# Head outputs evicted from PSUM by ScalarE instead of VectorE in a 56-unit attention stage

## The chip, the cores and the metric

The kernel runs on one core of one Trainium2 chip. The metric is device time in microseconds. Engines are named as in the profile: PE is TensorE (PEld its weight loads), DVE is VectorE, ACT is ScalarE, POOL is GpSimd, SP issues most DMAs.

## The reference

Two layers over 256 tokens of width 2048, all in fp32. Each layer is a projection, an attention stage with four kinds of heads, an output projection, a layer norm, a product-key expert layer over 16384 experts, and a second layer norm. Cut to what matters:

```python
def hybrid_mixer(x, w_in, sinks, lam_p, sub_g, w_out, layer_idx, cos, sin):
    proj = jnp.einsum('bld,dk->blk', x, w_in)
    ...
    oa = (acc * (corr / den)[..., None])      # A: 8 heads, window of 128, with sinks
    ob = diff_attention(...)                  # B: 4 heads of 128 columns, two softmaxes each
    ob = ob * lax.rsqrt(jnp.mean(jnp.square(ob), -1, keepdims=True) + RMS_EPS) * ...
    oc = num / den[..., None]                 # C: 8 heads, mixture of dilations
    od = dsa_attention(...)                   # D: 8 heads over the 64 keys an indexer picks
    mixed = jnp.concatenate([merge(oa), merge(ob), merge(oc), merge(od)], -1)
    return jnp.einsum('blk,kd->bld', mixed, w_out)
```

## The kernel before

Every weight matrix is streamed from HBM in tiles of 1 MB. ACT rounds each half tile to a high part (`split_hi`, L636), DVE forms the low part (`split_lo`, L919), and PE multiplies by both. These streams take nearly all of the time; the change touches only the attention stage between the input projection and the output projection, which runs once in each of the two layers.

The attention stage works through 56 units, one per head and block of 128 queries: 0 to 15 are the A heads, 16 to 23 the B heads, 24 to 39 the C heads, 40 to 55 the D heads. Even units have 128 keys, odd units 256. Each engine has its own list of instructions in program order, written out by hand, and semaphores tie them together. In step `u` of the loop the engines do this, in this order:

- PE: `scores(u+2)` (L442); `turn_probs(u)`: three transposes of the identity whose result nobody reads (L450), then the transposes of the probabilities (L456), which wait for the exponentials of unit u; `values(u-1)` (L469) into bank 6 or 7 by turns; and in units 0 to 15 `indexer_scores(u)` (L430) into the same two banks by turns.
- ACT: the exponentials of unit u+1 (L692, with a read of the accumulator, and in A units a sink term, L695); the copy of the transposed probabilities of unit u out of PSUM (L709); in units 0 to 15 the `relu` of the indexer's scores (L683), which waits for `indexer_scores(u)`; after unit 38 a square root; after units 40, 43, 46 and 49 one `split_hi` of the coming stream.
- DVE: mask and row maximum of unit u+1 (L1045), row sums of unit u (L1065, L1067 or L1071), the bias of the exponentials (L1053), the finishing of the probabilities with the reciprocal of the row sum (L1089), **the eviction of the output of unit u-2** (`take_out`, L1104 with 64 columns, L1100 with 128 for B heads), `indexer_add(u-1)` (L1005), a step of the indexer's top-k (L1028, L1030) at 17, 19, 21 and at every unit from 23 to 37, and a sum of squares (L1113) in units 28 to 35.

Two lines of PE say what waits for an eviction. In `indexer_scores(k)`, since it overwrites the bank in which the output of unit k-2 lies:

```python
if k >= 2:
    pe.wait_ge(irelu, k - 1)
    pe.wait_ge(head_out, k - 1)
```

and in `values(u)`, for the same reason, `pe.wait_ge(head_out, u - 1)`. `head_out` counts evicted outputs; with `k - 1` of them, unit k-2 has been evicted.

Of the kernel before, what the change touches and what calls it, by code (L numbers as in the profile page):

```python
# [20 lines left out]
HD = 64  # L21
# [67 lines left out]
def build(nc, x_in, w_in, w_out, wq, keys, u_t, v_t, ln, sinks, lamp, subg, layer_consts,  # L89
# [6 lines left out]
    with ExitStack() as ctx:  # L96
# [102 lines left out]
        def sem(name):  # L199
            s = ctx.enter_context(nc.semaphore(name))  # L200
            sems.append(s)
            return s
# [8 lines left out]
        scored, masked_done, nbias_done = sem("scored"), sem("masked_done"), sem("nbias_done")  # L211
        exp_done, sink_exp = sem("exp_done"), sem("sink_exp")
        mixed_probs, p_turned, p_stored = sem("mixed_probs"), sem("p_turned"), sem("p_stored")
        pv_done, head_out = sem("pv_done"), sem("head_out")
        rms_sum, rms_root, rms_scaled, mixed_done = sem("rms_sum"), sem("rms_root"), sem("rms_scaled"), sem("mixed_done")
        lam_sum, lam_exp = sem("lam_sum"), sem("lam_exp")
        out_evac = sem("out_evac")
# [32 lines left out]
        with nc.Fori(0, DEPTH) as layer:  # L250
# [7 lines left out]
            with nc.Block() as block:  # L258
# [367 lines left out]
                def _(act):  # L626
                    def split_hi(at, i, j, first=False):

                        if at == AT_IN and isinstance(i, int) and i == 0:
                            act.wait_ge(first_in[j // 2], layer * 16 + 16)  # L630
                        else:
                            act.wait_ge(raw_in[j // 2], i * 16 + at // BODY * 16)
                        if not first:
                            act.wait_ge(half_used, i * BODY + (at + j + 1 - NSPLIT))
                        half = raw[j // 2][:, (j % 2) * HT:(j % 2 + 1) * HT]
                        act.activation(hi[j % NSPLIT][:], half, ACT.Copy).then_inc(hi_done, 1)  # L636
# [48 lines left out]
                    def exps(u):  # L685
                        kind, h, b, items = UNITS[u]
                        K = (b + 1) * P
                        for n in items:
# [5 lines left out]
                            if kind == "A":  # L694
                                act.activation(small[:, 16 + n:17 + n], sinks_b[:, h:h + 1], ACT.Exp,  # L695
                                               bias=st[:, 1, n:n + 1]).then_inc(sink_exp, 1)

                    def unit_of(n):
                        return next(i for i, w in enumerate(UNITS) if n in w[3])

                    exps(0)
                    for u in range(n_units):
                        if u + 1 < n_units:
                            exps(u + 1)
                        K = (UNITS[u][2] + 1) * P
                        act.wait_ge(p_turned, u + 1)
                        if u >= 2:
                            act.wait_ge(pv_done, u - 1)
                        act.activation(probs_t[u % 2][:, 0:K], bank[4 + u % 2][:, 0:K], ACT.Copy).then_inc(p_stored, 1)  # L709
                        if u < N_IHEADS:  # L710
                            indexer_relu(u)
                        if u == AT_ROOT:

                            act.wait_ge(rms_sum, 8)
                            act.activation(small[:, 48:56], small[:, 40:48], ACT.Sqrt, bias=lay_b[:, 2:3],
                                           scale=1.0 / (2 * HD)).then_inc(rms_root, 1)
                        if u in SPLIT_UNITS:
                            split_hi(AT_OUT, 0, SPLIT_UNITS.index(u))
                    turn_high(1)
                    for m in range(NSPLIT, N_OUT):  # L720
                        split_hi(AT_OUT, m // BODY, m % BODY)
# [181 lines left out]
                def _(dve):  # L903
# [8 lines left out]
                    def own(n):  # L912
                        dve.wait_ge(dve_step, n)
# [138 lines left out]
                            dve.wait_ge(masked_done, i + 1)  # L1052
                            dve.tensor_scalar(st[:, 1, i:i + 1], st[:, 0, i:i + 1], -SCALE, None, ALU.mult).then_inc(nbias_done, 1)  # L1053

                    inverse = {}

                    def sums(u):

                        kind, h, b, items = UNITS[u]
# [13 lines left out]
                    def finish_probs(u, n):  # L1073

                        kind, h, b, items = UNITS[u]
                        K = (b + 1) * P
                        i = items[0]
                        if kind in "AB":
                            own(n)
                        if kind == "B":  # L1080
                            j = items[1]
                            own(mark(dve.tensor_scalar(probs[j % 4][:, 0:K], probs[j % 4][:, 0:K], st[:, 3, j:j + 1], neg_lam,
                                                       ALU.mult, ALU.mult)))
                            dve.scalar_tensor_tensor(out=probs[i % 4][:, 0:K], in0=probs[i % 4][:, 0:K], scalar=st[:, 3, i:i + 1],
                                                     in1=probs[j % 4][:, 0:K], op0=ALU.mult, op1=ALU.add).then_inc(mixed_probs, 1)
                            return
                        if kind == "C":
                            dve.wait_ge(mixed_probs, n_mixed(u))
                        inverse[u] = mark(dve.reciprocal(st[:, 3, i:i + 1], st[:, 2, i:i + 1]))  # L1089

                    def n_mixed(u):
                        return sum(UNITS[i][0] in "BC" for i in range(u + 1))

                    def take_out(u):
                        kind, h, b, items = UNITS[u]
                        dve.wait_ge(pv_done, u + 1)
                        src = bank[6 + u % 2]
                        if kind == "B":
                            at = MIX_B + 2 * HD * h
                            dve.tensor_copy(mixed[:, b, at:at + 2 * HD], src[:, 0:2 * HD]).then_inc(head_out, 1)  # L1100
                        else:
                            at = {"A": MIX_A, "C": MIX_C, "D": MIX_D}[kind] + HD * h
                            own(inverse[u])
                            dve.tensor_scalar(mixed[:, b, at:at + HD], src[:, 0:HD], st[:, 3, items[0]:items[0] + 1], None,  # L1104
                                              ALU.mult).then_inc(head_out, 1)


                    def square_sum(j):
                        h, b = j // 2, j % 2
# [14 lines left out]

                    row_max(0)
                    exp_bias(0)
                    for u in range(n_units + 2):
                        if u + 1 < n_units:
                            row_max(u + 1)
                        if u < n_units:  # L1130
                            n = sums(u)
                        if u + 1 < n_units:
                            exp_bias(u + 1)
                        if u < n_units:
                            finish_probs(u, n)
                        if u >= 2:
                            take_out(u - 2)
                        if 0 <= u - 1 < N_IHEADS:
                            indexer_add(u - 1)
                        if u in TOP_UNITS:  # L1140
                            top_round(TOP_UNITS.index(u))
                        if 0 <= u - AT_SQUARES < 8:
                            square_sum(u - AT_SQUARES)
                        if u == AT_ROOT + 3:
                            dve.wait_ge(rms_root, 1)
                            own(mark(dve.reciprocal(small[:, 40:48], small[:, 48:56])))
                        if 0 <= u - (AT_ROOT + 4) < 8:
                            rms_scale(u - (AT_ROOT + 4))
                        if u - 2 in SPLIT_UNITS:
                            split_lo(AT_OUT, 0, SPLIT_UNITS.index(u - 2))  # L1150
# [336 lines left out]
```

## Time and profile before

| | before |
|---|---|
| three timed runs | 4147.15, 4147.17, 4158.34 us; median 4147.17 |
| profiled execution | 4133.71 us, span 4131.7 us |
| PE busy | 3997.2 us (97%) |
| DVE busy | 2685.6 us (65%) |
| ACT busy | 1975.3 us (48%) |
| POOL busy | 516.8 us (13%) |

Busy time counts arithmetic, not semaphores or the issue of DMAs. The attention stage of the first layer lies between 246 and 343 us of the span, that of the second between 2326 and 2403 for its later units and a little before for the first ones. An engine's busy share over the whole span says little about that stage, in which the three engines hand small tiles to each other.

### The profile page before, as it was taken

The numbers are of one execution on the slowest core, as the hardware profiler recorded it, in microseconds if no ns is written. First come the engines' busy times: TensorE is split into PE (matmuls) and PEld (weight loads), VectorE is DVE, ScalarE is ACT, GpSimd is POOL, SyncE is SP. The second block draws the span as 40 slices with busy tenths as digits, with TensorE's granted clock in tenths as the row PEclk, the third lists the DMA queues.
The fourth block names the chain that finished last, engine by engine and source line by source line (L and its number), as shares of the span: only waits on it lengthen the run. The fifth ranks groups of instructions, "written<-read, shape, count | busy, mean of one in ns | idle before, by whom it ended". The sixth has DMA issues, their size and how long they took to land.

```text
span 4131.7 us, 65461 instructions
## 1 busy us (share of the span) xinstructions
PE 3997.2 (97%) x20692; PEld 3384.3 (82%) x20692; DVE 2685.6 (65%) x5308; ACT 1975.3 (48%) x2824; POOL 516.8 (13%) x728
## 2 busy tenths in 40 slices
PE   8999899999999999999899998999999999999997
PEld 7877788888888888888678777888888888888886
DVE  5665568667866555555656755686688665555556
ACT  4454344555455444444344543445554554444443
POOL 0100000451055000000001000004500540000000
PEclk9999999999999999999999998999999999999998
DMA  6523455558655666666445144555586456666664
GB/s 220 189 71 128 169 183 206 183 183 264 219 182 190 222 229 249 229 229 229 171 172 192 53 166 150 178 206 182 183 272 215 176 180 235 229 249 229 229 229 178
DMA packets 243055, 810.78 MB, mean 196 GB/s; under 512 B 24320, under 2 KB 157440, under 8 KB 157440
## 3 DMA queue, kind: packets, MB, share of 16 engines
q1 hardware_dynamic: 206080, 775.78, 53.6%
q10 hardware_dynamic: 36864, 33.57, 2.3%
q8 instruction: 64, 1.05, 0.1%
q14 instruction: 47, 0.39, 0.0%
HBM read 756.82 MB, written 52.43 MB: 196 GB/s over the span
## 4 chain that ended last, share of the span: by engine, by line
PE 43%; DVE 5%; issue 1%; ACT 1%; DVEq 0%; ACTq 0%
PE bank L371 10%; PE bank L592 6%; PE bank L594 6%; PE bank L593 6%; PE bank L372 5%; PE bank L383 2%; PE bank L385 2%; PE bank L384 2%; DVE lo L919 2%; PE bank L553 1%; DVE top_i L1248 0%; PE bank L450 0%; DVE top_v L1247 0%; DVE x L1182 0%; ACT hi L636 0%
## 5 line engine op out<-in xcount | busy, mean ns | idle before, releaser
L919 DVE TENSOR_TENSOR lo<-raw,hi 128x1024 fp32r<-128x1024 f32 x1312 | 1640.5, 1252 | 1197.5 <-ACT hi L636 1168.8
L636 ACT ACTIVATE hi<-raw 128x1024 fp32r<-128x1024 f32 x1312 | 1388.4, 1059 | 1369.7 <-PE bank L594 759.1
L371 PE MATMUL bank<-xhl,hi 128*128 128x512 f32 x4608 | 1642.7, 400 | 5.2 <-DVE xhl L925 2.8
L372 PE MATMUL bank<-xhl,lo 128*128 128x256 f32 x4608 | 1293.9, 281 | 0.0
L371 PEld LDWEIGHTS bank<-xhl,hi 128*128 128x128 f32 x4608 | 869.5, 189 | 211.0 <-DVE gelu_out L1225 3.9
L372 PEld LDWEIGHTS bank<-xhl,lo 128*128 128x128 f32 x4608 | 874.6, 190 | 0.0
L592 PE MATMUL bank<-hi,xhl 128*128 128x512 f32 x2048 | 797.1, 389 | 2.2 <-DVE gelu_out L1225 1.9
L593 PE MATMUL bank<-lo,xhl 128*128 128x512 f32 x2048 | 796.7, 389 | 0.0
L594 PE MATMUL bank<-hi,xhl 128*128 128x512 f32 x2048 | 796.7, 389 | 0.0
L592 PEld LDWEIGHTS bank<-hi,xhl 128*128 128x128 f32 x2048 | 384.4, 188 | 83.3 <-DVE gelu_out L1225 2.5
L594 PEld LDWEIGHTS bank<-hi,xhl 128*128 128x128 f32 x2048 | 384.4, 188 | 79.8
L593 PEld LDWEIGHTS bank<-lo,xhl 128*128 128x128 f32 x2048 | 384.4, 188 | 79.7
L866 POOL TENSOR_SCALAR scr<-iota_k,small 128x128 f32<-128x128 f32 x512 | 406.4, 810 | 12.3
L383 PE MATMUL bank<-hi,xhl 128*128 128x512 f32 (+1 forms) x896 | 353.1, 394 | 9.5 <-DVE lo L919 6.1
L385 PE MATMUL bank<-hi,xhl 128*128 128x512 f32 (+1 forms) x896 | 350.1, 391 | 0.0
L384 PE MATMUL bank<-lo,xhl 128*128 128x512 f32 (+1 forms) x896 | 350.1, 391 | 0.0
L876 POOL TENSOR_TENSOR x<-x,arena 128x512 f32<-128x512 f32 x8 | 13.4, 1681 | 1889.5 <-ACT x L733 1889.5
L756 ACT ACTIVATE gelu_out<-bank 128x256 f32<-128x256 f32 x256 | 97.0, 379 | 262.2 <-PE bank L372 262.0
L761 ACT ACTIVATE gelu_out<-gelu_out 128x256 f32<-128x256 f32 x256 | 105.9, 414 | 238.3 <-DVE gelu_out L1225 238.2
L383 PEld LDWEIGHTS bank<-hi,xhl 128*128 128x128 f32 x896 | 169.6, 189 | 43.8 <-issue 6.5
L385 PEld LDWEIGHTS bank<-hi,xhl 128*128 128x128 f32 x896 | 169.6, 189 | 34.7
L384 PEld LDWEIGHTS bank<-lo,xhl 128*128 128x128 f32 x896 | 169.8, 189 | 33.4
(133 smaller groups left out, 2592.2 us busy)
## 6 DMA issues: line engine op xcount, KB each, us to landing
raw<-u_t SPq DMA_DIRECT2D x256, 1024.0 KB, 4.8
raw<-v_t SPq DMA_DIRECT2D x256, 1024.0 KB, 4.8
raw<-w_in SPq DMA_DIRECT2D x84, 1024.0 KB, 4.8
raw<-w_out SPq DMA_DIRECT2D x32, 1024.0 KB, 4.8
raw<-wq SPq DMA_DIRECT2D x32, 1024.0 KB, 4.8
gelu_scratch<-gelu_out ACTq DMA_DIRECT2D x256, 128.0 KB, 1.7
scr<-gelu_scratch SPq DMA_DIRECT2D x256, 128.0 KB, 4.6
gates_scratch<-arena SPq DMA_DIRECT2D x32, 512.0 KB, 9.9
```

The lines of the kernel that those rows point to most:

```text
L371: pe.matmul(acc[:], wh, xhl[:, c, :, :].rearrange("p a t -> p (a t)"), start=(c == 0), stop=False)
L372: return pe.matmul(acc[:, L:2 * L], wl, xh[:, c, :], start=False, stop=(c == DC - 1))
L383: pe.matmul(banks[b][:, 0:width], st_h, mh, start=(c == first_c), stop=False)
L384: pe.matmul(banks[b][:, 0:width], st_h, ml, start=False, stop=False)
L385: last = pe.matmul(banks[b][:, 0:width], st_l, mh, start=False, stop=(c == last_c))
L592: pe.matmul(y, a_h, vh, start=start, stop=False)
L593: pe.matmul(y, a_h, vl, start=False, stop=False)
L594: last = pe.matmul(y, a_l, vh, start=False, stop=stop)
L636: act.activation(hi[j % NSPLIT][:], half, ACT.Copy).then_inc(hi_done, 1)
L761: act.activation(gelu_out[m % 2][:], gelu_out[m % 2][:], ACT.Gelu).then_inc(gelu_done, 1)
L866: last = pool.tensor_scalar(oh1[p][:, t, :], iota_k[:], key_cols[p][:, t:t + 1], None, ALU.is_equal)
L919: dve.tensor_tensor(lo[j % NSPLIT][:], half, hi[j % NSPLIT][:].bitcast(F32), ALU.subtract).then_inc(lo_done, 1)
```

## The change

`take_out` leaves DVE's list and enters ACT's. On ACT it stands in step u behind the copy of the transposed probabilities and ahead of the indexer's `relu`, and evicts unit u-2; the last two evictions follow the loop. For B heads it is a plain copy of 128 columns, for the others a copy of 64 columns whose scale is the column of reciprocals. The reciprocals stay on DVE and now count a semaphore, `inverted`, for which ACT waits. PE's list is the same.

```diff
+                    def take_out(u):
+                        kind, h, b, items = UNITS[u]
+                        act.wait_ge(pv_done, u + 1)
+                        src = bank[6 + u % 2]
+                        if kind == "B":
+                            at = MIX_B + 2 * HD * h
+                            act.activation(mixed[:, b, at:at + 2 * HD], src[:, 0:2 * HD], ACT.Copy).then_inc(head_out, 1)
+                        else:
+                            at = {"A": MIX_A, "C": MIX_C, "D": MIX_D}[kind] + HD * h
+                            act.wait_ge(inverted, n_inverted(u))
+                            act.activation(mixed[:, b, at:at + HD], src[:, 0:HD], ACT.Copy,
+                                           scale=st[:, 3, items[0]:items[0] + 1]).then_inc(head_out, 1)
...
                         act.activation(probs_t[u % 2][:, 0:K], bank[4 + u % 2][:, 0:K], ACT.Copy).then_inc(p_stored, 1)
+                        if u >= 2:
+                            take_out(u - 2)
                         if u < N_IHEADS:
                             indexer_relu(u)
...
+                    take_out(n_units - 2)
+                    take_out(n_units - 1)
                     turn_high(1)
...
-                        inverse[u] = mark(dve.reciprocal(st[:, 3, i:i + 1], st[:, 2, i:i + 1]))
+                        dve.reciprocal(st[:, 3, i:i + 1], st[:, 2, i:i + 1]).then_inc(inverted, 1)
...
-                        dve.wait_ge(pv_done, u + 1)
-                        src = bank[6 + u % 2]
...
-                            dve.tensor_copy(mixed[:, b, at:at + 2 * HD], src[:, 0:2 * HD]).then_inc(head_out, 1)
...
-                            own(inverse[u])
-                            dve.tensor_scalar(mixed[:, b, at:at + HD], src[:, 0:HD], st[:, 3, items[0]:items[0] + 1], None,
-                                              ALU.mult).then_inc(head_out, 1)
...
-                    for u in range(n_units + 2):
+                    for u in range(n_units):
...
-                        if u >= 2:
-                            take_out(u - 2)
```

ACT's list around units 8 and 9, as a difference from before (L709 of before is L725 now; L683 is the indexer's relu):

```order
 L695 ACTIVATE small<-par,st 128x1
-L709 ACTIVATE scr<-bank4 128x128
+L725 ACTIVATE scr<-bank4 128x128
+L711 ACTIVATE arena<-bank6,st 128x64
 L683 ACTIVATE scr<-bank6 128x256
 L692 ACTIVATE scr,st<-scr,st 128x128
 L695 ACTIVATE small<-par,st 128x1
-L709 ACTIVATE scr<-bank5 128x256
+L725 ACTIVATE scr<-bank5 128x256
+L711 ACTIVATE arena<-bank7,st 128x64
 L683 ACTIVATE scr<-bank7 128x256
```

The eviction has come in between the copy and the relu of each step. It reads the bank that the relu's own input is then written to.

PE's list at the same place, unchanged, with the semaphores that each instruction waits for:

```order
L456 MATMUL bank5<-ident,scr 128x128 [waits exp_done]
L456 MATMUL bank5<-ident,scr 128x128
L469 MATMUL bank6<-arena,scr 128x64 [waits irelu,head_out,p_stored]
L430 MATMUL bank7<-arena 128x256 [waits head_out,irelu]
L442 MATMUL bank0<-arena 128x128 [waits masked_done]
```

L430 waits for `head_out` as before, but what counts `head_out` now stands behind ACT's copy of the step; L442 and everything after it stand behind L430.

DVE's list in a C unit that also carries a top-k step and a sum of squares, before:

```order
L1067 SCALAR_TENSOR_TENSOR scr,st<-scr,arena 128x128
L1053 TENSOR_SCALAR st<-st 128x1
L1089 RECIPROCAL st<-st 128x1
L1104 TENSOR_SCALAR arena<-bank6,st 128x64
L1028 MAX small<-scr 128x8 x2
L1113 ISA scr,small<-arena 128x128
```

and now, where 20 lines have been added ahead of it (L1067 reads L1085, and so on):

```order
L1085 SCALAR_TENSOR_TENSOR scr,st<-scr,arena 128x128
L1073 TENSOR_SCALAR st<-st 128x1
L1107 RECIPROCAL st<-st 128x1
L1048 MAX small<-scr 128x8 x2
L1117 ISA scr,small<-arena 128x128
```

One instruction is gone, and nothing else has moved.

## Rows read from the trace of the kernel before

**Rows 1.** Windows, first layer's attention; engines' busy us (x instructions), then PEclk.

```profile
246.00:275.00 29.00, 28.51 (x194) 21.71 (x192) 21.26 (x123) 20.93 (x86) 0.00 (x0) 1.00 0.00 1
275.00:290.00 15.00, 12.39 (x80) 8.16 (x79) 14.34 (x79) 9.90 (x38) 0.00 (x0) 1.00 0.01 2
290.00:318.00 28.00, 26.24 (x161) 19.25 (x161) 26.97 (x176) 13.98 (x49) 0.00 (x0) 1.00 0.00 1
```

**Rows 2.** Timeline, units 9 to 11: start us, duration us, engine, line.

```profile
263.31 0.37 ACT L709 ACTIVATE scr<-bank 128x256 f32<-128x256 f32 x1
...
263.33 0.48 PE L430 MATMUL bank<-arena 64*128 64x256 f32 x1
...
264.06 0.38 ACT L683 ACTIVATE scr<-bank 128x256 f32<-128x256 f32 x1 [0.38 <-PE bank L430]
...
264.34 0.50 ACT L692 ACTIVATE scr<-scr,st 128x256 f32<-128x256 f32 x1
...
265.02 0.26 ACT L709 ACTIVATE scr<-bank 128x128 f32<-128x128 f32 x1
...
265.15 0.70 PE L430 MATMUL bank<-arena 64*128 64x256 f32 x2
...
266.59 0.38 PE L456 MATMUL bank<-ident,scr 128*128 128x128 f32 x2
...
267.01 0.39 ACT L709 ACTIVATE scr<-bank 128x256 f32<-128x256 f32 x1 [0.18 <-PE bank L456]
```

**Rows 3.** Timeline, unit 2's indexer and what follows; last row: unit 15's indexer.

```profile
252.06 0.49 PE L430 MATMUL bank<-arena 64*128 64x128 f32 x2
...
252.58 0.28 ACT L683 ACTIVATE scr<-bank 128x128 f32<-128x128 f32 x1 [0.39 <-PE bank L430]
252.75 0.39 ACT L692 ACTIVATE scr<-scr,st 128x128 f32<-128x128 f32 x1
...
253.71 0.39 ACT L709 ACTIVATE scr<-bank 128x256 f32<-128x256 f32 x1 [0.29 <-PE bank L456]
...
274.25 0.48 PE L430 MATMUL bank<-arena 64*128 64x256 f32 x1
```

**Rows 4.** Groups by form, ACT, attention of the first layer: busy us, mean ns.

```profile
L692 ACT ACTIVATE scr<-scr,st 128x256 f32<-128x256 f32 x32 | 16.1, 503 | 11.6 <-DVE st L1053 11.6
L692 ACT ACTIVATE scr<-scr,st 128x128 f32<-128x128 f32 x32 | 12.7, 397 | 9.7 <-DVE st L1053 9.4
...
L709 ACT ACTIVATE scr<-bank 128x128 f32<-128x128 f32 x28 | 7.3, 261 | 0.3 <-PE bank L456 0.3
```

**Rows 5.** Timeline, DVE in unit 30: eviction and the instruction after it.

```profile
301.47 0.28 DVE L1104 TENSOR_SCALAR arena<-bank,st 128x64 f32<-128x64 f32 x1
...
301.67 0.28 DVE L1028 MAX8 small<-scr 128x8 f32<-128x128 f32 x1
```

**Rows 6.** Timeline, ACT's copies of units 24, 28 and 36.

```profile
292.09 0.26 ACT L709 ACTIVATE scr<-bank 128x128 f32<-128x128 f32 x1
...
298.21 0.25 ACT L709 ACTIVATE scr<-bank 128x128 f32<-128x128 f32 x1
...
313.21 0.26 ACT L709 ACTIVATE scr<-bank 128x128 f32<-128x128 f32 x1
```

**Rows 7.** Timeline, PE, the identity transposes of units 41 and 43.

```profile
321.32 0.31 PEld L450 LDWEIGHTS bank<-ident 128*128 128x128 f32 x3 [0.33 <-issue]
...
324.20 0.31 PEld L450 LDWEIGHTS bank<-ident 128*128 128x128 f32 x3 [0.33 <-issue]
```

**Rows 8.** Timeline, the square root after unit 38 and PE's wait behind it.

```profile
316.38 1.28 ACT L715 ACT_TABLE_LOAD   x1
...
319.83 0.14 PEld L456 LDWEIGHTS bank<-ident,scr 128*128 128x128 f32 x1 [1.41 <-ACT scr L692]
```

**Rows 9.** Timeline, unit 47's copy, the next exponential, and `values(47)` on PE.

```profile
331.29 0.37 ACT L709 ACTIVATE scr<-bank 128x256 f32<-128x256 f32 x1
...
331.61 0.51 ACT L692 ACTIVATE scr<-scr,st 128x256 f32<-128x256 f32 x1
...
331.71 0.41 PEld L469 LDWEIGHTS bank<-arena,scr 128*128 128x128 f32 x3
```

**Rows 10.** Windows, around the first layer norm: columns as in Rows 1.

```profile
440.00:445.00 5.00, 0.00 (x0) 0.00 (x0) 4.47 (x10) 2.40 (x5) 2.27 (x2) 0.72 0.00 0
445.00:450.00 5.00, 2.48 (x11) 2.14 (x12) 5.00 (x4) 1.19 (x2) 4.24 (x3) 0.50 0.00 0
```

More of the change, by code:

```diff
@@ L213, in build @@
         mixed_probs, p_turned, p_stored = sem("mixed_probs"), sem("p_turned"), sem("p_stored")
-        pv_done, head_out = sem("pv_done"), sem("head_out")
+        pv_done, inverted, head_out = sem("pv_done"), sem("inverted"), sem("head_out")
         rms_sum, rms_root, rms_scaled, mixed_done = sem("rms_sum"), sem("rms_root"), sem("rms_scaled"), sem("mixed_done")
@@ L696, in exps, with n_inverted @@
                                                bias=st[:, 1, n:n + 1]).then_inc(sink_exp, 1)
+                    def n_inverted(u):
+                        return sum(UNITS[i][0] != "B" for i in range(u + 1))
+                    def take_out(u):
[10 more added lines that the diff above has]
+                                           scale=st[:, 3, items[0]:items[0] + 1]).then_inc(head_out, 1)
                     def unit_of(n):
@@ L1053, in exp_bias @@
                             dve.tensor_scalar(st[:, 1, i:i + 1], st[:, 0, i:i + 1], -SCALE, None, ALU.mult).then_inc(nbias_done, 1)
-                    inverse = {}
                     def sums(u):
@@ L1088, in finish_probs @@
                             dve.wait_ge(mixed_probs, n_mixed(u))
-                        inverse[u] = mark(dve.reciprocal(st[:, 3, i:i + 1], st[:, 2, i:i + 1]))
+                        dve.reciprocal(st[:, 3, i:i + 1], st[:, 2, i:i + 1]).then_inc(inverted, 1)
                     def n_mixed(u):
                         return sum(UNITS[i][0] in "BC" for i in range(u + 1))
-                    def take_out(u):
-                        kind, h, b, items = UNITS[u]
-                        dve.wait_ge(pv_done, u + 1)
-                        src = bank[6 + u % 2]
-                        if kind == "B":
-                            at = MIX_B + 2 * HD * h
-                            dve.tensor_copy(mixed[:, b, at:at + 2 * HD], src[:, 0:2 * HD]).then_inc(head_out, 1)
-                        else:
-                            at = {"A": MIX_A, "C": MIX_C, "D": MIX_D}[kind] + HD * h
-                            own(inverse[u])
-                            dve.tensor_scalar(mixed[:, b, at:at + HD], src[:, 0:HD], st[:, 3, items[0]:items[0] + 1], None,
-                                              ALU.mult).then_inc(head_out, 1)
                     def square_sum(j):
```

## The prediction

> **What bounds the kernel now.** I read the page first: PE is busy for 97% of the span, so time is won or lost only where PE waits or can be made to wait. The change touches the attention stage alone, so I cut that stage of the first layer into windows by kind of unit. In units 0 to 15 PE is busy for 28.51 of 29 us and is the bound. In the B units DVE is busy for 14.34 of 15 us and PE for 12.39; in units 23 to 38 DVE has 26.97 of 28 us, PE 26.24 and ACT only 13.98 [rows 1]. There DVE is the bound, or close to PE. So the work leaves an engine that matters from unit 16 on, and does not matter before.
>
> Then I read the timeline for what stands between the engines. In units 0 to 15 PE starts the indexer's scores of unit 9 at 263.33, almost together with ACT's copy at 263.31, and ACT's relu waits for them [rows 2]. Nothing that ACT does in that step holds PE back. That is what the change ends: `head_out` for unit u-2 was counted by DVE, long before PE came to `indexer_scores(u)`, and is now counted by ACT behind the copy of step u, which itself waits for PE's transposes of step u. PE must stand at L430 until ACT has copied and evicted, and everything behind L430 on PE (the scores, transposes and values of the next unit) stands with it.
>
> **The cost of one eviction on ACT.** No row shows a 64-column copy with a column as scale. An exponential, which also has a column as operand, takes 503 ns for 256 columns and 397 for 128 [rows 4]: 64 columns fewer are 53 ns less, so 0.34 us, which I take, since it has the same kind of operand. The lower bound is the plain copy from PSUM, 261 ns for 128 columns [rows 4], less the same 53: 0.21. The upper bound is the 128-column exponential itself, 0.40. For ACT's own list less counts, because an instruction starts about 0.10 us before the end of the one ahead (the relu of 0.28 at 252.58 is followed at 252.75 [rows 3]): 0.24.
>
> The Trainium skill, "ScalarE: Activation LUTs", section "What ACT_TABLE_LOAD costs", gives an ACTIVATE with immediate operands 186 ns plus 0.833 ns per column and each column operand 93 ns more. By that this one would take 0.33 us, an estimate from the page; at 128 columns with one such operand it gives 0.39, and the trace agrees with 397 ns. It would change the sum by 0.01 us in each of 14 units.
>
> **Units 2 to 15: a new loop.** The time from one `indexer_scores` to the next now runs: the scores, the relu, the next exponentials, the next copy, the eviction, and the signal to PE. The parts, for 256 indexer columns: scores to relu 0.73 (263.33 to 264.06), relu to exponential 0.28, exponential to copy 0.68 before an even unit's copy [rows 2], and 0.11 less before an odd one, by the difference of the two exponentials. For 128 columns: 0.52 and 0.17 [rows 3]. From the start of a copy to the next instruction on ACT I take 0.16 for 128 columns (0.26 less 0.10) and 0.32 for 256 (331.29 to 331.61 [rows 9]); then 0.34 for the eviction and 0.05 from ACT's end to PE's start (331.66 to 331.71 [rows 9]). So the tail from copy to `indexer_scores` is 0.55 into an even unit and 0.71 into an odd one.
>
> There is a second way round, through PE: from `indexer_scores(u)` over the next scores and transposes to the next copy. Where the scores use the same rows of the array as the indexer, the way into an odd unit is the longer: 265.15 to 267.01, 1.86 us [rows 2], or 252.06 to 253.71, 1.65 us, with 128 columns [rows 3]. Where they use different rows, ACT's way is longer. This makes, per unit:
>
> - 256 columns: three into even units, 0.73 + 0.28 + 0.68 + 0.55 = 2.24; two into odd ones by ACT's way, 0.73 + 0.28 + 0.57 + 0.71 = 2.29; two by PE's way, 1.86 + 0.71 = 2.57. Sum 16.4.
> - 128 columns: three even, 0.52 + 0.17 + 0.68 + 0.55 = 1.92; one odd by ACT's way, 1.97; two by PE's way, 1.65 + 0.71 = 2.36. Sum 12.4.
>
> Together 28.8 us for 13 steps, against 274.25 - 252.06 = 22.2 us now [rows 3]: 6.6 more. Unit 2 has a first stall of its own, about 0.4 by the same parts. So **+7.0 us per layer**, and ACT, PE and DVE are all late by it when the B units start, since the exponentials of unit 17 follow the relu of unit 15.
>
> **Units 16 to 38: DVE gives some back.** From the eviction's start to the next instruction DVE takes 0.20 us (301.47 to 301.67 [rows 5]); its own duration of 0.28 overlaps. In units 28 to 35, with top-k step and sum of squares, DVE has no gap: eight units take 15.00 us (298.21 to 313.21 [rows 6]), 3.75 a pair, while PE needs 2.88 a pair where nothing holds it (321.32 to 324.20 [rows 7]). All eight evictions count: 1.6. In units 24 to 27 a pair takes 3.06 (292.09 to 298.21 [rows 6]), so only 0.18 a pair can be had before PE's 2.88; with the pair before it 0.5. In the B units every second unit waits for the exponentials' end before its second row maximum, and DVE's list is the bound only in the other half: 4 x 0.20 = 0.8, with both ends 0 and 1.6. ACT's evictions fit in its idle time there: it is busy for 13.98 of 28 us [rows 1], and 16 x 0.24 is 3.8. So **-2.9 us per layer**. Without that idle time these evictions would cost up to 3.8.
>
> **Unit 38 to the end.** The square root's table load at 316.38 stands behind the eviction of unit 36, and PE waits for the exponential behind it at 319.83 [rows 8]: 0.24 later, less about 0.2 that a lighter DVE wins before it. `values(39)` and `values(47)` start right at the end of a copy (331.66 to 331.71 [rows 9]) and now also wait for the eviction behind it: 0.3 to 0.4 each. In the other D units PE is the bound and ACT is ahead. The last units, without scores on PE, run at the pace of copy and values: 0.4. Together **+1.1 us per layer**, with both ends 0 and 2.2.
>
> **Sum.** 7.0 - 2.9 + 1.1 = 5.2 us per layer, 10.4 us for both. The profiled execution would go from 4133.71 to 4144.1; the median of the timed runs stands 13.5 us above it, so the median becomes 4157.6 us, 0.25% more. A measurement of this kernel can tell about 0.3%, 12.4 us, from no change.
>
> **The rivals.**
>
> 1. The wait is hidden: the stall at L430 costs nothing because something else holds PE as long. It would need a second wait at the same place. The 0.18 and 0.29 us that ACT's copy waits for PE's transposes [rows 2, 3] show the opposite: PE is what ACT waits for, and it has 0.5 us idle in 29 [rows 1]. It would leave -2.9 + 1.1 per layer, so 4143.6.
> 2. Faster: the relief of DVE counts in every unit and ACT's new work lies in ACT's waits. For it: DVE's busy share from unit 16 on, and the 0.38 us that ACT waits for L430 [rows 2]. Then 112 x 0.20 = 22.4 us are won, 4124.8. It decides only if the eviction ends before PE reaches L430. ACT's copy of unit 9 starts when PE starts L430 [rows 2], so the eviction would have to come before the copy, which the order of ACT's list rules out.
> 3. Slower by clock: PE, now waiting in every unit, loses its full clock. At the first layer norm PE had nothing to do for 5 us, and the granted clock was 0.72 and then 0.50, the lower of its two levels of 1.2 and 2.4 GHz [rows 10]. Against it: in the B units PE was busy 12.39 of 15 us, in waits of under 1 us, at 1.00 [rows 1], and the new waits make it 28.5 of 36, much the same share. It decides once the rows show a clock under 0.9 in units 2 to 15. PE's 28.5 us of work there would double, some 20 us a layer beyond its waits: 4197. The Trainium skill, "TensorE: Matmul & The Clock Gate", Part 1, has the clock follow recent activity; [rows 1, 10] agree.
> 4. The same mechanism, but with no gift from DVE, because PE and ACT take over as bounds as soon as DVE is lighter: 7.0 + 1.1 per layer, 4163.4.
>
> **How the numbers follow.** My forecast, with cases of its size on both sides of it, 0.72; rival 1, 0.07; rival 2, 0.04; rival 3, 0.03; rival 4, 0.14. Bounds of the forecast: an eviction of 0.21 takes 13 x 2 x 0.13 + 0.3 = 3.7 us off, one of 0.40 adds 1.7; B units between 0 and 1.6 per layer move it by 1.6 either way; the last part between 0 and 2.2 by 2.2 either way. That makes 4150.1 to 4163.1. The range reaches on to rival 4 and a little beyond for the spread of the runs, 4148 to 4166. Over 0.3% slower is more than 4159.6: about 0.3 of the forecast's 0.72, all of rivals 3 and 4: 0.39. Faster by over 0.3% is rival 2 alone, 0.04. The rest, 0.57, is within 0.3%.
>
> **What would show it.** In the profile after, windows for units 0 to 15 would show some 36 us instead of 29 with PE busy about 28.5 and a clock of 1.00; the waits would have a row of L430, or its weight load, waiting for ACT's L711, some 0.5 us long, 14 times per layer; L711 would have a mean near 0.34 us. Units 28 to 36 would take about 13.4 us instead of 15.0. I am wrong if L430 waits for nothing, if its waits don't lengthen the units, or if the C units don't get shorter; and the size is off if L711's duration is nearer 0.21 or if unit 38's table load moves by more than 0.3.

## The result and the profile after

| | before | after |
|---|---|---|
| median of six timed runs | 4148.24 us (4147.15 to 4158.34) | 4185.31 us (4173.08 to 4192.14) |
| ratio, 95% interval | | 1.0083 (1.0061 to 1.0104) |
| profiled execution, mean granted clock | 4133.71 us, 0.985 | 4185.17 us, 0.973 |

The kernel became slower by 0.83%, 37 us where 10.4 were forecast, and the time lies outside the range. First the page of after: its span, its busy times and the row of PE's granted clock in 40 slices.

```profile
span 4183.2 us, 65461 instructions
...
PE 4041.1 (97%) x20692; PEld 3421.8 (82%) x20692; DVE 2666.6 (64%) x5196; ACT 2001.5 (48%) x2936; POOL 515.4 (12%) x728
...
PEclk9998899999999999999999989999999999999998
```

PE has the same 20692 instructions as before and is busy for 43.9 us more (4041.1 - 3997.2). No PE instruction was added, so PE ran more slowly somewhere. The clock row has an 8 in its fourth slice, 314 to 418 us, in which the first layer's attention stage ends; before's row has a 9 there.

I then cut the first layer's stage by units, from the start of ACT's copy of one unit to that of another: from the copy of unit 0 to that of unit 15, then to those of 23, 38, 40 and 55. Below I call these windows the A units, the B units, the C units, the wait at unit 40 (its copy comes right behind that wait) and the D units. These are the windows of before; the columns are the stretch, its length, busy time (instructions) of PE, PEld, DVE, ACT and POOL, PE's granted clock, DMA share and GB/s.

```profile
249.65:274.19 24.54, 24.38 (x170) 19.16 (x169) 18.86 (x106) 18.08 (x78) 0.00 (x0) 1.00 0.00 1
274.19:290.70 16.51, 13.90 (x92) 9.52 (x90) 15.85 (x90) 10.30 (x41) 0.00 (x0) 1.00 0.01 2
290.70:316.11 25.41, 23.65 (x145) 17.14 (x143) 25.09 (x164) 12.13 (x45) 0.00 (x0) 1.00 0.00 1
316.11:320.51 4.40, 3.23 (x21) 2.28 (x20) 1.78 (x12) 4.34 (x10) 0.00 (x0) 1.00 0.00 0
320.51:341.18 20.67, 20.67 (x141) 16.62 (x140) 16.79 (x83) 14.71 (x49) 0.00 (x0) 1.00 0.26 90
```

The same units in after:

```profile
249.86:284.66 34.80, 28.91 (x171) 22.30 (x169) 17.00 (x99) 20.97 (x90) 0.00 (x0) 0.86 0.00 1
284.66:302.64 17.98, 16.40 (x92) 12.02 (x91) 14.03 (x76) 11.64 (x48) 0.00 (x0) 0.79 0.00 1
302.64:325.14 22.50, 22.09 (x144) 17.06 (x142) 21.91 (x150) 15.38 (x61) 0.00 (x0) 1.00 0.01 2
325.14:329.90 4.76, 3.31 (x21) 2.32 (x19) 1.48 (x10) 4.70 (x12) 0.00 (x0) 0.98 0.00 0
329.90:367.50 37.60, 37.60 (x142) 30.16 (x141) 14.75 (x68) 17.82 (x65) 0.00 (x0) 0.50 0.15 56
```

The clock was 1.00 in all of before's stretches. Now it is 0.86, 0.79 and, in the D units, 0.50, half speed, which is 1.2 GHz in place of 2.4. The D units alone take 37.60 us instead of 20.67. The A units take 10.3 us more, of which a part is the stall that was forecast. Only the C units got shorter, as was thought, by 2.9 us. Lateness counts from the same copy in before. In the second layer the copy of unit 55 comes 53.7 us late and that of unit 0 27.6 us, so it lost 26.1 us too; the first lost 26.3.

The forecast stall stands in the timeline of after, units 10 and 11, and can be read against [rows 2].

```profile
269.43 0.26 ACT L725 ACTIVATE scr<-bank 128x128 f32<-128x128 f32 x1
...
269.59 0.31 ACT L711 ACTIVATE arena<-bank,st 128x64 f32<-128x64 f32 x1
...
270.04 0.67 PE L430 MATMUL bank<-arena 64*128 64x256 f32 x2 [0.41 <-ACT arena L711]
...
270.75 0.38 ACT L683 ACTIVATE scr<-bank 128x256 f32<-128x256 f32 x1 [0.85 <-PE bank L430]
```

Copy, eviction, PE's L430, and then ACT's own relu behind it: the loop of the prediction. By unit 12 ACT's copy is 5.5 us late, 5.3 of it since unit 0, all of it at full clock. Then the clock falls, in unit 13 (windows of after):

```profile
272.00:274.00 2.00, 1.40 (x11) 1.25 (x10) 0.59 (x6) 1.15 (x5) 0.00 (x0) 1.00 0.00 0
274.00:276.00 2.00, 1.59 (x10) 0.84 (x9) 0.83 (x6) 0.84 (x6) 0.00 (x0) 0.78 0.03 8
276.00:280.00 4.00, 3.55 (x16) 3.01 (x17) 1.56 (x7) 2.25 (x10) 0.00 (x0) 0.50 0.01 2
290.00:295.00 5.00, 5.00 (x32) 3.90 (x32) 3.89 (x24) 3.05 (x13) 0.00 (x0) 0.78 0.00 0
328.00:330.00 2.00, 0.67 (x3) 0.51 (x4) 0.42 (x4) 1.99 (x8) 0.00 (x0) 0.93 0.00 0
330.00:332.00 2.00, 2.00 (x7) 1.23 (x7) 0.35 (x4) 1.70 (x5) 0.00 (x0) 0.50 0.00 0
340.00:350.00 10.00, 10.00 (x38) 7.78 (x37) 5.43 (x21) 5.22 (x19) 0.00 (x0) 0.50 0.29 107
```

It comes back near 292, in the B units, and falls again just before 330. What PE did there is in the timeline around unit 40:

```profile
325.64 1.28 ACT L733 ACT_TABLE_LOAD   x1
...
328.55 0.40 ACT L692 ACTIVATE scr<-scr,st 128x128 f32<-128x128 f32 x1
...
329.09 0.33 PE L456 MATMUL bank<-ident,scr 128*128 128x128 f32 x1 [1.21 <-ACT scr L692]
...
329.66 1.04 PE L469 MATMUL bank<-arena,scr 128*128 128x64 f32 x4 [0.24 <-ACT arena L711]
...
331.77 0.90 PE L450 MATMUL bank<-ident 128*128 128x128 f32 x3
```

PE waits 1.21 us for the exponential behind the table loads, then 0.24 more for an eviction. The 1.41 us of [rows 8] are those of a weight load; the row of before that can be set beside these is that of PE:

```profile
319.84 0.33 PE L456 MATMUL bank<-ident,scr 128*128 128x128 f32 x1 [1.17 <-ACT scr L692]
```

In before no wait for an eviction follows. So from the copy of unit 38 to that of unit 40 PE is without work for 1.17 us in before and for 1.45 us in after. The three transposes of the identity took 0.55 us with the clock at 1.00 and take 0.90 here: the half clock. PE is busy for 10.00 of 10 us from 340 to 350, and the clock stays at 0.50.

What each eviction cost is close to what was foreseen. By its source line, in after:

```profile
L711 ACT ACTIVATE arena<-bank,st x96: 302/308/318, 252.3 to 2454.4; 128x64 f32<-128x64 f32 x96
...
  PE bank L430: 12.4, 26
  PE bank L469: 1.7, 4
```

The median is 308 ns. PE's L430 waited for it 26 times in two layers, 0.48 us each.

### The profile page after: what moved, and what is told of

Its sections match the earlier page's. It is cut to its first block and busy times, and to the rows that moved or that the text cites. A ratio compares the mean times of both kernels' runs of the same rounds, so it can differ in the third digit from the quotient of the medians.

```text
span 4183.2 us, 65461 instructions
## 1 busy us (share of the span) xinstructions
PE 4041.1 (97%) x20692; PEld 3421.8 (82%) x20692; DVE 2666.6 (64%) x5196; ACT 2001.5 (48%) x2936; POOL 515.4 (12%) x728
## 5 line engine op out<-in xcount | busy, mean ns | idle before, releaser
L383 PEld LDWEIGHTS bank<-hi,xhl 128*128 128x128 f32 x896 | 169.6, 189 | 43.9 <-issue 6.6
```

The lines of the kernel that those rows point to most:

```text
L383: pe.matmul(banks[b][:, 0:width], st_h, mh, start=(c == first_c), stop=False)
```

## The experiments

The theory that I took to the chip: the prediction's three terms hold, and the rest is PE's clock, lost in two places for two reasons. The idle times of units 2 to 15 do the one, the wait at unit 40 the other. The rivals were: the units grew for another reason and the clock only went with it; the clock falls because ACT evicts in the D units; and the D fall is a consequence of the one in the A units.

Times are medians; "before" stands for the kernel before, timed beside them 26, 26 and 17 times: 4147.98 for the first four kernels, 4147.99 for the next four, 4147.67 for the last three.

| run | median, us (lowest to highest, runs) | ratio to before, 95% | clock, profiled |
|---|---|---|---|
| e1_fill_A | 4171.00 (4169.27 to 4172.85, 5) | 1.0052 (1.0029 to 1.0076) | 0.978 |
| e2_fill_A_40 | 4138.94 (4135.37 to 4142.63, 10) | 0.9974 (0.9963 to 0.9985) | 0.987 |
| e3_early | 4151.27 (4132.27 to 4161.34, 10) | 1.0004 (0.9988 to 1.0021) | 0.985 |
| e4_A_on_dve | 4155.96 (4153.73 to 4159.27, 10) | 1.0018 (1.0002 to 1.0033) | 0.977 |
| e5_A_on_act | 4191.16 (4173.37 to 4193.94, 4) | 1.0096 (1.0066 to 1.0127) | 0.971 |
| e6_before_fill_40 | 4133.39 (4131.29 to 4138.00, 12) | 0.9969 (0.9954 to 0.9984) | 0.986 |
| e7_early_fill_40 | 4131.07 (4127.54 to 4134.53, 12) | 0.9967 (0.9955 to 0.9979) | 0.987 |
| e8_A_on_dve_fill_40 | 4126.67 (4124.99 to 4130.96, 9) | 0.9955 (0.9939 to 0.9971) | 0.988 |
| e9_more_in_D | 4175.89 (one execution) | | 0.979 |
| e10_after_fill_40 | 4157.26 (4151.77 to 4167.24, 10) | 1.0027 (1.0007 to 1.0046) | 0.980 |
| e11_only_16_37 | 4122.23 (4119.92 to 4127.49, 6) | 0.9934 (0.9913 to 0.9954) | 0.988 |

**Filling PE's waits: e1_fill_A, e2_fill_A_40, e10_after_fill_40.** e1 adds four transposes of the identity, which nobody reads, ahead of the wait at L430 in units 2 to 15. e10 leaves that out and puts 14 such transposes instead of 3 ahead of the wait at unit 40 (`AT_ROOT` is 38). e2 has both.

```diff
 # e1, e2: indexer_scores
+for _ in range(4 if k >= 2 else 0):
+    pe.transpose(bank[4 + (k + 1) % 2][:, W - P:W], ident[:], ident[:])
 # e2, e10: turn_probs
-for _ in range(3):
+for _ in range(14 if u == AT_ROOT + 2 else 3):
```

> The changed kernel with four more identity transposes on PE ahead of each indexer score of units 2 to 15, into a bank that nobody reads; they lie in the wait for ACT's eviction. Theory 'wait and clock': the units 2 to 15 keep a granted clock of 1.00 in both layers; the stalls themselves stay (about 7 us a layer more than before), but the 5 to 7 us a layer that PE loses there at half clock are gone; the D units, whose clock falls after unit 38, lose as much as in the changed kernel. Median about 4172 us. Rival 'waits alone': the clock is a side effect, the fillers only lengthen PE's list: 4185 us or more, with half clock still in units 13 to 17. A third outcome, if the fall in the D units is an aftermath of the one in the A units: both go, 4158 us.

> As the run before, and fourteen instead of three identity transposes on PE ahead of unit 40, where PE waits about 1.2 us for the exponential behind the table load. Theory 'wait and clock': the D units keep a clock of 1.00 too, and 26 to 28 us for both layers come back: about 4158 us, what the stalls alone were forecast to give. Rival, if the wait at unit 40 is not what lets the clock fall: D units at half clock as before, time equal to the run before.

> The changed kernel with fourteen transposes ahead of unit 40 and nothing in units 2 to 15. Theory 'wait and clock': the falls of the D units and of the A units are two separate ones. The D units keep 1.00 and give back some 15 us a layer; the A units still fall, 5 to 6 us a layer. Median about 4139 + 11 = 4150 us, granted clock 0.86 in units 0 to 15. Rival 'one chain': the D units still fall, since the A units did; 4180.

e1 took 14.3 us off after's time, and e10 28.1. The windows of e2, first layer, by the same units as above:

```profile
249.71:281.30 31.59, 30.42 (x224) 23.74 (x223) 15.99 (x92) 20.75 (x90) 0.00 (x0) 1.00 0.00 1
281.30:297.86 16.56, 14.16 (x96) 9.89 (x94) 14.91 (x83) 11.65 (x49) 0.00 (x0) 1.00 0.00 1
297.86:320.36 22.50, 22.09 (x144) 17.06 (x142) 21.91 (x150) 15.38 (x61) 0.00 (x0) 1.00 0.01 2
320.36:325.12 4.76, 4.51 (x32) 3.52 (x31) 1.47 (x10) 4.70 (x11) 0.00 (x0) 1.00 0.01 3
325.12:346.68 21.56, 21.16 (x142) 16.79 (x141) 13.96 (x68) 17.42 (x64) 0.00 (x0) 1.00 0.28 98
```

More work on PE, and the kernel is 46 us shorter than after: what the idle times did to the clock cost more than the idle times as such. Every eviction is where the change put it, and the clock is 1.00 throughout. So the second rival, ACT's evictions in the D units, falls. So does the first: with 56 transposes more, the A units take 31.59 us, not 34.80.

Of e1 the rows of the A units, of the wait at unit 40 and of the D units:

```profile
249.82:281.41 31.59, 30.41 (x224) 23.74 (x223) 15.99 (x92) 20.75 (x91) 0.00 (x0) 1.00 0.01 2
320.46:325.22 4.76, 3.31 (x21) 2.32 (x20) 1.47 (x10) 4.70 (x11) 0.00 (x0) 1.00 0.00 0
325.22:361.26 36.04, 36.04 (x142) 28.97 (x141) 14.65 (x68) 17.83 (x65) 0.00 (x0) 0.53 0.17 59
```

And of e10 those of the A and of the D units:

```profile
248.90:286.38 37.48, 32.14 (x171) 24.80 (x169) 17.02 (x99) 21.10 (x91) 0.00 (x0) 0.77 0.00 1
...
331.61:353.17 21.56, 21.16 (x142) 16.79 (x141) 13.97 (x68) 17.42 (x64) 0.00 (x0) 1.00 0.28 98
```

In e1 the A units kept the clock and the D units lost it; in e10 it was the other way round. So the D units fall without a fall in the A units, against the third rival.

**Who evicts where: e4_A_on_dve, e5_A_on_act.** Both give a set of units back to DVE, in DVE's old place, and leave the others on ACT; the second is the complement of the first.

```diff
+ON_DVE = range(0, 16)      # e5: range(16, 56)
...
-                        if u >= 2:
+                        if u >= 2 and u - 2 not in ON_DVE:
                             take_out(u - 2)
...
+                        if u >= 2 and u - 2 in ON_DVE:
+                            take_out_dve(u - 2)
```

> Only the evictions of units 16 to 55 are moved to ACT; those of units 0 to 15 stay on DVE. Theory 'wait and clock': units 0 to 15 as before, clock 1.00, no stall; units 16 to 38 win 3 to 4 us a layer; so about 4141 us, or 4167 us if the clock falls at unit 40 by itself. Rival 'waits alone': the evictions on ACT in the later units cost what they cost in the changed kernel, 26 us or more for both layers, with no fall of the clock.

> The other half: the evictions of units 0 to 15 on ACT, those of units 16 to 55 on DVE as before. Theory 'wait and clock': units 2 to 15 and the B units cost what they cost in the changed kernel, 12 to 13 us a layer, 7 of them stalls and the rest half clock; the D units, whose list on ACT is that of before, lose nothing if their fall came from the later evictions, so about 4147 + 25 = 4172 us. If the D units' clock depends only on the wait at unit 40, which this kernel has as well, it can fall there too, by chance of where it stands: up to 4195.

With the A evictions on DVE the A units took 24.53 us at 1.00, as before, so the stall and its clock fall belong to those evictions. The D units lost the clock all the same. In the windows of e4 (unit 40 starts at 317.03):

```profile
316.00:318.00 2.00, 1.54 (x7) 1.16 (x7) 0.74 (x7) 2.00 (x9) 0.00 (x0) 0.81 0.00 0
318.00:320.00 2.00, 2.00 (x9) 1.45 (x7) 1.14 (x6) 0.92 (x4) 0.00 (x0) 0.50 0.00 0
320.00:330.00 10.00, 10.00 (x37) 7.78 (x38) 5.23 (x22) 4.74 (x17) 0.00 (x0) 0.50 0.00 0
```

In e5 the D evictions were on DVE, the wait at unit 40 was before's in the first layer (PE busy for 3.23 of 4.40 us), and yet:

```profile
247.25:287.08 39.83, 35.40 (x170) 27.47 (x169) 17.04 (x99) 21.38 (x90) 0.00 (x0) 0.68 0.00 1
...
335.47:371.37 35.90, 35.90 (x141) 28.84 (x140) 18.78 (x83) 14.96 (x49) 0.00 (x0) 0.52 0.17 59
```

So even before's arrangement can fall in the D units. That led to the next runs. In the second layer of e5 the clock fell sooner, in unit 37, ahead of the square root:

```profile
2412.00:2414.00 2.00, 1.55 (x11) 1.13 (x11) 1.97 (x15) 0.87 (x4) 0.00 (x0) 1.00 0.00 0
2414.00:2416.00 2.00, 2.00 (x11) 1.60 (x11) 1.98 (x12) 1.11 (x5) 0.00 (x0) 0.76 0.00 0
```

PE's waits there, of up to 0.45 us, are for DVE, as in before, whose C units kept the clock in both layers of its profiled execution. So the wait at unit 40 is not the only place at which this stage can fall.

The A units have the same lists in after, e10, e9 and e5, and lose the clock at different times: in the first layer near 275 us in after (unit 13), near 269 in e10 (unit 11) and near 261 in e5 (unit 8). The sooner it fell, the longer they took: 34.80, 37.48 and 39.83 us.

**Does before itself lose the clock there? e6_before_fill_40, e8_A_on_dve_fill_40.** The 14 transposes at unit 40 (the second diff above) go into before, and into e4.

> The kernel before with fourteen instead of three identity transposes on PE ahead of unit 40. Theory: the spread of the kernel before, 4132 to 4163 us, is the clock falling in some executions after the wait at unit 40, for which its profiled execution of 4133.7 us is one without a fall. Then this kernel stays near the lower end: median 4133 to 4138, spread under 10 us, 0.3% faster than before. Rival: its spread comes from elsewhere, and the fill changes nothing (4148).

> Evictions of units 0 to 15 on DVE, those of units 16 to 55 on ACT, and the fourteen transposes ahead of unit 40. Theory: no stall in units 0 to 15, 3.3 us a layer won in units 16 to 38, 1.2 given back after them, no fall of the clock: 4 to 5 us under the kernel before with the same fill, about 4129 us, the fastest of all. Rival: the D units fall to half clock from the new waits behind the copies and not from the wait at unit 40; then 4156 as without the fill.

The kernel before gained 0.31% from eleven idle transposes, and e4 29.3 us. In e6 PE has no gap left at the wait; its row for the stretch from the copy of unit 38 to that of unit 40 reads:

```profile
313.71:318.11 4.40, 4.40 (x32) 3.48 (x31) 1.78 (x12) 4.34 (x11) 0.00 (x0) 1.00 0.00 0
```

The 69 runs of before fall into three groups: 17 from 4131.0 to 4138.4 at a mean clock of 0.984 to 0.986, 40 from 4143.7 to 4151.5 at 0.980 to 0.983, 12 from 4157.4 to 4165.6 at 0.977 to 0.980. Their means are 12.9 and 12.6 us apart. All twelve of e6 lie from 4131.3 to 4138.0, in the first group. So before loses the clock at unit 40 in neither, one or both of its layers, and one loss costs about 13 us. This is inferred from e6 and from the clocks: no profiled execution of before shows a fall, and in the traces of other kernels a fall lengthened the D units by 14.5 to 16.0 us. The profiled execution of before, 4133.71 us, on which the whole prediction was built, was one without any.

**The order on ACT: e3_early, e7_early_fill_40.** The eviction of unit u-2 goes ahead of the copy of unit u in ACT's list; it brings the wait for `pv_done` with it. e7 has the 14 transposes too.

```diff
-                        act.wait_ge(p_turned, u + 1)
-                        if u >= 2:
-                            act.wait_ge(pv_done, u - 1)
-                        act.activation(probs_t[u % 2][:, 0:K], bank[4 + u % 2][:, 0:K], ACT.Copy).then_inc(p_stored, 1)
                         if u >= 2:
                             take_out(u - 2)
+                        act.wait_ge(p_turned, u + 1)
+                        act.activation(probs_t[u % 2][:, 0:K], bank[4 + u % 2][:, 0:K], ACT.Copy).then_inc(p_stored, 1)
```

> The changed kernel with one move on ACT: the eviction of unit u-2 stands ahead of the copy of unit u, not behind it. Theory 'wait and clock': the stall of PE at the indexer score is gone, since the eviction no longer stands behind PE's transposes of the same unit; units 0 to 15 take 29 us a layer as before with clock 1.00, units 16 to 38 are 3 to 4 us shorter. If the D units' fall has its own cause at unit 40, they still lose 13 us a layer: about 4166 us; if it follows from the A units, about 4141 us. Rival 'ACT is too full': units 0 to 15 stay 5 us or more longer than before, since ACT's list is the bound.

> The early eviction on ACT (ahead of the copy) with the fourteen transposes ahead of unit 40. Theory: the traces of the early kernel stand 1.4 us a layer below the kernel before where no clock fell, and its spread of 4132 to 4161 us came from falls; with the fill the median is 4131 to 4136 us. Rival: the falls of the early kernel come from its units 0 to 15, where PE is busy for 24.96 of 27.45 us and not 24.38 of 24.54; then the spread stays and the median is near 4150.

In the timeline of e3, unit 12:

```profile
269.21 0.30 ACT L711 ACTIVATE arena<-bank,st 128x64 f32<-128x64 f32 x1
...
269.40 0.27 ACT L725 ACTIVATE scr<-bank 128x128 f32<-128x128 f32 x1
...
269.65 0.45 PE L430 MATMUL bank<-arena 64*128 64x256 f32 x1 [0.24 <-ACT arena L711]
```

The wait is 0.24 us instead of the 0.41 of after's unit 12, the A units take 27.45 us instead of 34.80, and they keep the clock. The stall was expected to be gone; it is only smaller, since before's A units took 24.54. The runs of e3 still spread from 4132.3 to 4161.3, and its median equals that of before. With the wait at unit 40 filled, e7, the highest run is 4134.5, so the spread came from the fall there. The median of e7 is 2.3 us under that of e6, but not through this stage: from the copy of unit 0 to that of unit 55 it takes 91.62 us in e7 and 91.54 in e6.

**What keeps the clock down in the D units? e9_more_in_D.** Five more idle transposes in each unit from 41 on, and none more at unit 40, so that the clock may fall as in after.

```diff
-for _ in range(3):
+for _ in range(3 if u <= AT_ROOT + 2 else 8):
```

> The changed kernel with eight instead of three identity transposes in each unit from 41 on and no fill at unit 40: can more work of the full array bring the clock back where the D units have fallen to the lower level with PE busy all the time? If it is the kind of work that keeps the level low, the clock is back at 1.00 a few units after the fall and units 40 to 55 take about 28 us, not 37.6. If not, they stay at 0.50 and take 37.6 + 15 x 5 x 0.11 x 2 = 54 us.

Windows of e9 behind its unit 40:

```profile
330.00:335.00 5.00, 3.55 (x15) 2.39 (x14) 1.44 (x12) 4.08 (x12) 0.00 (x0) 0.73 0.00 0
335.00:340.00 5.00, 5.00 (x25) 4.59 (x24) 2.12 (x7) 1.62 (x7) 0.00 (x0) 0.59 0.00 0
340.00:345.00 5.00, 5.00 (x37) 4.08 (x37) 2.44 (x11) 3.08 (x11) 0.00 (x0) 1.00 0.01 5
```

The clock fell near 332 and was back near 339. From the copy of unit 40 to that of unit 55 it took 31.97 us, with 75 more transposes, against 37.60; in the second layer 31.69 against 37.59. PE was busy for nearly all of the time in both kernels; what differed was what it was busy with. It is one execution, though with the same course in both layers.

**The version that follows: e11_only_16_37.** ACT evicts only units 16 to 37, where DVE is the bound; DVE keeps the others, and unit 40 has its 14 transposes.

```diff
+ON_DVE = [*range(0, 16), *range(38, 56)]
```

> Evictions on ACT in units 16 to 37 alone, on DVE in the others, and the fourteen transposes ahead of unit 40. Theory: the gain of units 16 to 38 stays (3.3 us a layer), the 1.2 us a layer that ACT's evictions cost from unit 38 on are gone: about 2 us under the version with only units 0 to 15 on DVE, 4124 to 4126 us. Rival: DVE's evictions in the D units cost what ACT's do; 4127, no difference.

It is 0.66% faster than before. Its D units:

```profile
317.19:338.00 20.81, 20.81 (x142) 16.76 (x141) 17.09 (x85) 14.71 (x49) 0.00 (x0) 1.00 0.26 90
```

That is 0.75 us less a layer than in e2, where `values` waited for evictions on ACT. About 15 of its 25 us come from the filled wait (e6: 14.6 us), which has nothing to do with the change. The evictions that were moved where they help shorten the stage by 2.81 us a layer against before's profiled execution (88.72 us from the copy of unit 0 to that of unit 55, against 91.53), 5.6 for both. The other 5 us or so lie outside the stage and are not explained.

**What was expected and missed.** e1, e6 and e7 came where they were expected. e2 came 19 us under its 4158, e4 11 us under its 4167 and e3 between its two numbers. These had been reckoned from before's median of 4147, which has the clock falls in it; without them before takes 4133. e10 came 7 us over its 4150, since the fall in its A units cost more than was allowed for. e8 and e11 came 2.3 and 1.8 us under, e5 near its upper end of 4195, and the D units of e9 took 32 us, not 28.

## Why the prediction was wrong

**The three terms were right in kind, and their sum was.** e2 is the change without a clock fall, with four idle transposes a unit added, which had lengthened it by 0.2 us at unit 12 (5.48 us late, 5.29 in after). Its copies against before's in the first layer, counted from unit 0: 7.7 us late at unit 16, where the B units start (forecast 7.0), 4.2 at unit 38 (so -3.5; forecast -2.9), 5.4 at unit 55 (so +1.25; forecast +1.1), together 5.4 a layer against 5.2. Both layers make 11.0 at the last unit. By medians against e6 it is only 5.6, and the profiled span is 9.1 longer than before's (4140.8 against 4131.7). The streams outside the stage differ by several us from kernel to kernel: from the end of the first layer's stage to the start of the second's (copy of unit 55 to copy of unit 0) it is 1962.5 us in e11 and 1970.7 in e6. I did not follow that up.

**So two terms were off and made up for each other:** the loop by 0.7 us a layer, what DVE gives back by 0.6. In e4, where no stall comes before them, units 16 to 38 won 3.3, and two sizes within that were off: the B units won 0.4 a layer, not 0.8, and units 28 to 35 won 2.3, not 1.6. Units 24 to 27 with the pair before them won 0.5, as forecast.

**The eviction** took 308 ns, not 0.34 us, well inside its bounds. The estimate of 0.33 from the Trainium skill, "ScalarE: Activation LUTs", section "What ACT_TABLE_LOAD costs", was nearer by 0.01 us and still 0.02 above the measurement.

**Two steps failed. The one in the A units was the dismissal of rival 3**, at a chance of 0.03. It compared PE's busy share in the new A units ("28.5 of 36 much the same share") with that of the B units, which had kept the clock. e1 and e2 show the same units at full clock once the gaps are filled, and after, e5, e9 and e10 lose it in units 0 to 15 of both layers (0.67 to 0.86). The price was mis-sized too: in after the clock lasts to unit 13 and comes back in the B units, so the fall cost 14.3 us (after against e1) to 18.3 (e10 against e2), not 40. The share itself was foreseen well: up to the copy of unit 12, still at full clock, PE was busy for 19.37 of 24.41 us in after (0.79, as 28.5 of 36). But the share did not tell a stretch that falls from one that does not. Before's B units had 13.90 of 16.51 (0.84) and kept the clock. In the second layer of e5 PE had been busy for 19.39 of 21.35 us (0.91) from the copy of unit 24 to that of unit 36, and the clock fell right behind it, in unit 37; before's same units, with 19.35 of 21.11, kept it.

The Trainium skill has a case of this kind in "TensorE: Matmul & The Clock Gate", section "A second HAM failure mode: psum-queue depth-cycling": a kernel whose TensorE idles briefly between groups of matmuls goes back and forth between the two levels. The trace of after agrees: the waits of L430 in units 0 to 15 of the first layer come to 5.7 us in 12 waits, the longest of 0.6 us. I had drawn on the page's Part 1 only for a long pause.

**The other step that failed is the term "Unit 38 to the end", +1.1 us a layer.** It costed unit 38's table load at 0.24 us less 0.2, took the PE-bound units behind it at full clock and stopped there. Those units, from the copy of unit 40 to that of unit 55, take 37.60 us at half clock and 21.56 at full, so the term was not 1.1 but 17.3 us a layer (after's copies are 8.8 us late at unit 38 and 26.1 at unit 55, counted from unit 0). These falls cost 28.1 us (after against e10) to 32.1 (e1 against e2), the larger part of everything.

**The offset to the median was the same fall.** I carried the 13.5 us between before's profiled execution and its median over as a constant. By e6 it was one fall behind the wait at unit 40, and the first row to doubt: three timed runs at 4147 and 4158 beside a profiled one at 4134.

The parts, in medians, along a path from before to after: before without its falls, 4147.99 to 4133.39, -14.6; the moved evictions without any fall, e6 to e2, +5.6; D falls, e2 to e1, +32.1; A falls, e1 to after, +14.3. That makes 37.4, and 37.1 was measured; it is a sum of differences that closes by its making, so what it shows is the sizes. The six runs of after spread from 4173.1 to 4192.1, so the last part is known to some us only.

**Of the rivals:** 1 is refuted by the 26 waits of L430, 2 by the order that it was refused for, 4 by C units of 22.50 us. 3 was right in kind, at another place and price.

**What stays open.** Why the fall at unit 40 came in every profiled layer where units 24 to 37 were evicted by ACT behind the copy and the wait was not filled (after, e1, e4, e9), but only in some runs of before and e3. One difference stands in the traces: from the copy of unit 38 to that of unit 40 PE was without work for 1.45 us in seven of those eight layers (1.30 in the second of e9, whose clock fell before the second wait would have come), for 1.17 in before and the first layer of e5, and for 1.19 to 1.20 in e3. The 0.24 us that PE waits there for ACT's eviction are the change's own. Whether that difference decides was not tried; a run that fills it alone would tell. With the wait filled PE was still without work for 0.25 us there (e2, e8, e10, e11), and none of their eight layers fell. It is also open why the C units of e5 fell in the second layer, and why the A units fall in unit 8 of one run and in unit 13 of another.

## What to carry to other kernels

An eviction that another engine waits for must not stand in its new queue behind work which itself waits for that engine; count the loop that this closes before counting the relief. Move evictions by stretch, not all at once: here it paid only where the old engine was the bound. And where a clock of 1.00 carries a stage, look at the clock beside the time of every run, not only at the profiled one, before taking any offset as constant; if the runs fall into groups, find the wait behind them and fill it with idle transposes, which at unit 40 cost nothing that shows (91.54 us from the copy of unit 0 to that of unit 55 in e6, 91.53 in before) and were worth 0.31% in a kernel that nobody had changed.

## What the runs showed of the hardware

- The clock of PE can stay at 0.50 for 37 us with PE busy 10.00 of 10 us in the profile (after, D units). The Trainium skill, "TensorE: Matmul & The Clock Gate", section "What's actually happening", has activity release the throttle. In these traces the profile's busy time does not tell when that comes: the same units with five more 128x128 transposes of the identity each had the clock back after some 7 us, in both layers (e9).
- A wait of 1.2 us in a stage that has run at 1.00 until then can be followed by half clock for the next 37 us (e4, where 0.24 us more came behind it) or for most of the next 36 (the first layer of e5, with 1.17), or not (the profiled execution of before, with 1.17).
- Waits of up to 0.6 us, nearly one a unit, were followed by half clock from unit 8 (e5, near 261 us), 11 (e10, near 269) or 13 (after, near 275) on. Eight waits of up to 0.4 us (e3, 2.2 us together) and seven of up to 0.2 us (e2, 1.1 us together) in these units were not.
- Idle transposes of the identity in a wait kept the clock at 1.00 where it had fallen without them: in the A units of e1 and e2, and behind unit 40 in e2, e8 and e10.
